# One layer of four recurrent mixers and one layer of three attentions: the gate's gelu moved and rewritten, and the last block of the memory's projection read in another order of rows

## The chip, the cores and the metric

The kernel runs on one core of one Trainium2 chip. The metric is the device time of one launch in microseconds (us), the median of several launches. Five engines work in parallel, each on its own queue of instructions in program order: TensorE (PE in the profile; PEld is its loading of weights), VectorE (DVE), ScalarE (ACT), GpSimd (POOL) and SyncE (SP, which here issues most of the DMA). An engine waits for another by a semaphore, and everything behind a waiting instruction in its own queue waits too.

## What is computed

256 tokens of width 2048 go through two blocks. The first block normalises x, projects it with `w_in` to the inputs of four mixers (gated DeltaNet, mLSTM, RG-LRU, RWKV-7), joins their outputs, projects with `w_out`, and adds a gated feed-forward network. The second block has three attentions (MoBA, dilated, memory) and a gated merge. The parts that the change touches are these:

```
def rglru_block(u, conv_w, conv_b, w_a, b_a, w_x, b_x, lam):
    xb, gate = jnp.split(u, 2, axis=-1)
    xb = causal_conv(xb, conv_w) + conv_b
    ...
    a = jnp.exp(log_a)
    inp = jnp.sqrt(-jnp.expm1(2.0 * log_a)) * (i * xb.astype(jnp.float32))
    _, h = lax.associative_scan(linear_scan_combine, (a, inp), axis=1)
    return h * jax.nn.gelu(gate.astype(jnp.float32))
...
    mix = jnp.concatenate([y.astype(x.dtype) for y in (y_gdn, y_mlstm, y_rglru, y_rwkv)], axis=-1)
    x = x + mix @ w_out[l]
...
        mkv = jnp.einsum('bmd,de->bme', mem_n, w_mem_kv[layer])
```

## The kernel before

Every large matrix product is a list of **blocks** of 512 (or twice 256) columns, and a block a list of **steps**, one for each 128 rows k of the weights. The products are in fp32 precision by splitting both operands into a high and a low part: in mode N (lines 653 to 655) a step is six matmuls 128x512, high by high, low by high, high by low, for two tiles of tokens. SyncE loads weights into `raw` (three units), ScalarE casts each half of a unit to `ringH` (line 1362), VectorE subtracts to get `ringL` (line 1983); the rings hold four halves of two steps each. The results in the two PSUM pairs `pp` are drained by ScalarE (line 1423 for the memory's values) or VectorE. The blocks' order is fixed: RWKV's inputs, mLSTM's, DeltaNet's, the RG-LRU's gate `r1` and its input `r0`, the memory's keys and values `kv0` to `kv3`, then the output projection `o0.3` to `o3.3`, `o0.1` and so on, whose number behind the dot is the mixer that it reads. A block can have a gate: `o0.3` may not begin before the stage `mix3` is open.

Beside the blocks run the **stages**, the small work of the mixers. Each stage is a generator that yields at points where other work may go in between. `course` puts the two together, in the same way for each engine. In the stretch of interest its line is

```
    L.weave(L.both(L.stage("gdn"), small_mixers(L), "rwkv"), 3.5)
```

so DeltaNet's stage is advanced by one piece, then `small_mixers` by one piece, and then `weave` gives TensorE as many steps of the blocks as the piece's pace says (3 to 5), which fill the time in which VectorE and ScalarE answer the small matmuls. If the next step's gate is closed, no step is given. DeltaNet's small matmuls are: the inversion of its triangular matrices in five levels, each with a first product (line 801, 16 of 64x64, drained by VectorE line 2260), then the second and third (line 801, 32 of 64x32, drained by lines 2268 and 2273); the join of halves (lines 865 and 871, drained by lines 2316 and 2321); and the two chunks of the recurrence (line 1171, drained by ScalarE 1780; 1178, drained by 2679; 1164, drained by 2668, 2672 and 2657; 1171 again), then the outputs (1189, 1190).

`small_mixers` holds in this order: the RG-LRU (`rglru`: per half of two tiles the convolution 2515, two products 1213, sigmoids 1816, tanh 1823, exp 1828, square 1831 and square root 1834 on ScalarE, 2716 to 2732 on VectorE), the load of x for the residual (`xload`), and then `mix3`: the splitting of RWKV's output (tiles 12 to 15 of `mix`) into high and low parts in `nS` (ScalarE 1842, VectorE 2739). `nS` holds the memory until `kv3` has read it, so `mix3` comes behind the whole of `kv3`, and all of its pieces at once (`L.run("mix3")`).

The gelu of the RG-LRU's gate lies inside `rglru`: a square on ScalarE (1802), two operations on GpSimd (2964, 2966), a tanh on ScalarE (1826) and two more on GpSimd (2976, 2978), all 128x1024 f32.

Of the kernel before, what the change touches and what calls it, by code (L numbers as in the profile page):

```python
# [9 lines left out]
ACT = mybir.ActivationFunctionType  # L10
# [6 lines left out]
T = 256  # L17
# [300 lines left out]
def program(nc, I, out):  # L318
    ctx = ExitStack()
    with ctx:  # L320
# [26 lines left out]
        def v3(o, a, b):  # L347
            return AR[:, o:o + a * b].rearrange("p (a b) -> p a b", a=a)
# [142 lines left out]
        def block(tag, W, nk, cols, x, mode="M", gate=None, by="A"):  # L491
            if mode == "M" and cols == 512:
                for name, c in (("." + tag, slice(0, 256)), (tag, slice(256, 512))):
                    block(name, W[:, c], nk, 256, x, mode, gate, by)
                return
            pos = 0
            B = Block(len(blocks), tag, W, nk, cols, mode, x, by)
            blocks.append(B)
            for u in range(0, nk, 2048 // cols):
                nu = min(2048 // cols, nk - u)  # L500
                units.append((W[128 * u:128 * (u + nu), :].rearrange("(k p) n -> p k n", p=128), nu, cols))
                for h in range(0, nu, 1024 // cols):
                    nh = min(1024 // cols, nu - h)
                    halves.append((len(units) - 1, h, nh, cols, h + nh >= nu))
                    for kk in range(nh):
                        k = u + h + kk
# [84 lines left out]
        def tensor(e, S, ring, lane):  # L591
# [527 lines left out]
            def gdn(L):  # L1119
# [77 lines left out]
                yield 5  # L1197

            def rglru(L):
                yield  # L1200
# [122 lines left out]
            def attB(L):  # L1323
# [11 lines left out]
                "norm": norm, "gates": gates, "scan": scan, "fold": fold, "lambda": lam, "stat2": stat2, "mem": mem, "rwkv": rwkv, "mlstm": mlstm, "gdn": gdn,  # L1335
                "rglru": rglru, **{f"mix{m}": split(4) for m in range(4)}, **{f"split1.{q}": split1(q) for q in range(4)},
                **{f"split2.{q}": split2(q) for q in range(4)}, "xf": split(8), "attA": attA, "attM": attM, "attB": attB,
                **{f"ysplit.{n}": ysplit(n) for n in range(5)}, "mgsplit.0": mgsplit(0, 12), "mgsplit.1": mgsplit(12, 16)}))

        def scalar(e, S, ring, lane):  # L1340
# [388 lines left out]
            def gdn(L):  # L1729
# [63 lines left out]
                yield  # L1793

            def rglru(L):
                Lp, Ln = small[:, 40:44], small[:, 48:52]
                yield
                L.upto("r0")
                GA = v3(MU, 4, T)
                e.wait_ge(*ml_v.at("end"))  # L1800
                e.wait_ge(*pool.at("r1"))
                act(GA, mix[:, 8:12, :], ACT.Square).then_inc(*rg_a.tick("sq"))
                X, Rr, Ii, Aa, Th = (v3(RU + 1040 + 512 * k, 2, T) for k in range(5))
                for hf in range(2):
# [17 lines left out]
                    for j in range(2):  # L1822
                        t = act(Th[:, j, :], Rr[:, j, :], ACT.Tanh, scale=Lp[:, 2 * hf + j:2 * hf + j + 1])
                    if hf == 0:
                        e.wait_ge(*pool.at("gl"))
                        act(GA, GA, ACT.Tanh, scale=float(np.sqrt(2.0 / np.pi))).then_inc(*rg_a.tick("th"))
                    for j in range(2):
# [107 lines left out]
            def final(L):  # L1935
# [11 lines left out]
                "norm": norm, "scan": scan, "mem": mem, "fold": fold, "lambda": lam, "rwkv": rwkv, "mlstm": mlstm,  # L1947
                "gdn": gdn, "rglru": rglru,
                **{f"mix{m}": split("mix", nS, lambda k: mix[:, k, :], range(4 * m, 4 * m + 4), mix_ready) for m in range(4)},
# [7 lines left out]
        def vector(e, S, ring, lane):  # L1957
# [636 lines left out]
            def gdn(L):  # L2594
# [107 lines left out]
                yield  # L2702

            def rglru(L):
                e.memset(rU[:, :, 0:3], 0.0).then_inc(*rg_v.tick("pad"))
# [4 lines left out]
                for hf in range(2):  # L2710
# [18 lines left out]
                    yield  # L2729
                    e.wait_ge(*pool.at("ge"))  # L2730
                    own(rg_v)
                    tt2(mix[:, 8 + 2 * hf:10 + 2 * hf, :], GA[:, s2, :], Th, MUL).then_inc(*rg_v.tick(hf, "end"))
                    yield
# [126 lines left out]
            def attB(L):  # L2860
# [6 lines left out]
            course(lane(unit, {  # L2867
                "norm": norm, "gates": gates, "scan": scan, "mem": mem, "fold": fold, "lambda": lam, "rwkv": rwkv, "mlstm": mlstm, "gdn": gdn, "rglru": rglru,
                **{f"mix{m}": split("mix", nS, lambda k: mix[:, k, :], range(4 * m, 4 * m + 4)) for m in range(4)}, "stat1": stat1,
# [6 lines left out]
        def gpsimd(e, S, ring, lane):  # L2876
# [81 lines left out]
            def rglru(L):  # L2958
                X, Rr, Ii, Aa, Th = (v3(RU + 1040 + 512 * k, 2, T) for k in range(5))
                GA, g = v3(MU, 4, T), mix[:, 8:12, :]  # L2960
                yield
                L.upto("r0")
                e.wait_ge(*rg_a.at("sq"))
                e.tensor_scalar(GA, GA, 0.044715, 1.0, MUL, ADD).then_inc(*pool.tick())
                e.wait_ge(*pool.now())
                e.tensor_tensor(GA, GA, g, MUL).then_inc(*pool.tick("gl"))
                for hf in range(2):
                    yield
                    yield
                    e.wait_ge(*rg_v.at("cv", hf, 1))  # L2970
                    e.wait_ge(*rg_a.at(hf, "g", 1))
                    e.tensor_tensor(Ii, Ii, X, MUL).then_inc(*pool.tick("ix", hf))
                    yield
                    if hf == 0:
                        e.wait_ge(*rg_a.at("th"))
                        e.tensor_scalar(GA, GA, 0.5, 0.5, MUL, ADD).then_inc(*pool.tick())
                        e.wait_ge(*pool.now())
                        e.tensor_tensor(GA, GA, g, MUL).then_inc(*pool.tick("ge"))
                    yield
                    yield  # L2980
                    yield
# [231 lines left out]
```

## Time and profile before

| | us |
|---|---|
| median of 3 runs | 2418.83 (2418.06 to 2420.80) |
| the profiled execution, whole | 2422.39 |
| its span in the profile | 2420.6 |
| TensorE busy | 2391.7 (99%) |
| VectorE busy | 1451.6 (60%) |
| ScalarE busy | 1131.5 (47%) |
| GpSimd busy | 104.1 (4%) |

The profile is one execution recorded by the hardware. "Busy" counts the time in which at least one instruction of the engine runs. A line of the timeline gives start, duration, engine, line of the kernel, operation, output and input, a count, and in brackets the idle time before it and what ended that. Lines that run back to back are merged with a count. A matmul row of count 32 at line 801 is 16 products of the program, each recorded as two passes.

### The profile page before, as it was taken

The page shows a single profiled execution, that of the slowest core. Times are in us where ns is not written, and L with a number is a line of the kernel's source. Part 1 is how long each engine was busy: PE and PEld are TensorE (multiplying, and loading weights), DVE is VectorE, ACT ScalarE, POOL GpSimd, SP SyncE. Part 2 cuts the span into 40 slices and gives each one's busy share as a digit, 9 for nine tenths or more (in the row PEclk, how much of TensorE's full clock was granted, in tenths as well). Part 3 has the DMA queues.
Part 4 walks back from the last instruction along what each step waited for, and adds up shares of the span by engine and source line. Part 5 has one row for each costly group of instructions (what it writes and reads, how often), then busy time and mean ns, then how long its engine had stood idle before and what let it go on. Part 6 is the DMA issues. An engine that isn't in the chain of part 4 may idle for free.

```text
span 2420.6 us, 32301 instructions
## 1 busy us (share of the span) xinstructions
PE 2391.7 (99%) x13432; PEld 1990.9 (82%) x13432; DVE 1451.6 (60%) x1860; ACT 1131.5 (47%) x1425; POOL 104.1 (4%) x81
## 2 busy tenths in 40 slices
PE   9999999999999999999999999999999999999998
PEld 7777888978888888888888888888888888888887
DVE  6777657678755555555555565555555655555555
ACT  6635435563554444434443464445444455444444
POOL 1000001320000000000000040000000000000000
PEclk9999999999999999999999999999999999999999
DMA  9633334645555555555555566555445544555564
GB/s 298 224 123 122 123 123 162 234 162 184 196 192 184 185 190 188 195 189 184 184 190 191 181 213 232 188 177 168 163 157 191 191 140 157 192 191 192 192 240 140
DMA packets 245329, 443.55 MB, mean 183 GB/s; under 512 B 7360, under 2 KB 72512, under 8 KB 242624
## 3 DMA queue, kind: packets, MB, share of 16 engines
q1 hardware_dynamic: 241984, 423.65, 53.2%
q0 software_dynamic: 2624, 17.30, 1.9%
q8 instruction: 107, 1.75, 0.3%
q10 hardware_dynamic: 576, 0.53, 0.1%
q14 instruction: 38, 0.31, 0.0%
HBM read 430.97 MB, written 10.49 MB: 182 GB/s over the span
## 4 chain that ended last, share of the span: by engine, by line
PE 95%; DVE 2%; ACT 1%; DMA 1%; issue 0%; SPq 0%; ACTq 0%; DVEq 0%
PE pp L653 25%; PE pp L655 24%; PE pp L654 24%; PE pp L682 8%; PE pp L683 4%; PE ps L612 2%; PE ps L1274 1%; PE ps L1288 1%; PE ps L801 1%; DVE ringL L1983 1%; DMA mem_hold<-memSt 1%; DMA raw<-in_w_in 0%; PE ps L854 0%; ACT ringH L1362 0%; PE pp L688 0%
## 5 line engine op out<-in xcount | busy, mean ns | idle before, releaser
L1983 DVE TENSOR_TENSOR ringL<-raw,ringH 128x1024 fp32r<-128x1024 f32 x779 | 963.3, 1243 | 687.8 <-ACT ringH L1362 686.3
L1362 ACT CAST ringH<-raw 128x1024 fp32r<-128x1024 f32 x779 | 814.6, 1050 | 994.9 <-PE pp L655 870.3
L653 PE MATMUL pp<-ringH,nS 128*128 128x512 f32 x1376 | 544.0, 395 | 1.1 <-DVE nS L2739 1.1
L655 PE MATMUL pp<-ringH,nS 128*128 128x512 f32 x1376 | 536.4, 390 | 0.0
L654 PE MATMUL pp<-ringL,nS 128*128 128x512 f32 x1376 | 535.9, 389 | 0.0
L682 PE MATMUL pp<-nS,ringH 128*128 128x512 f32 x992 | 367.9, 411 | 8.7 <-DVE ringL L1983 4.5
L655 PEld LDWEIGHTS pp<-ringH,nS 128*128 128x128 f32 x1376 | 258.3, 188 | 54.4
L653 PEld LDWEIGHTS pp<-ringH,nS 128*128 128x128 f32 x1376 | 258.5, 188 | 54.0 <-ACT AR L1423 1.2
L654 PEld LDWEIGHTS pp<-ringL,nS 128*128 128x128 f32 x1376 | 258.6, 188 | 51.3 <-issue 0.2
L683 PE MATMUL pp<-nS,ringL 128*128 128x256 f32 x992 | 281.4, 284 | 0.0
L653 PE MATMUL pp<-ringH,xS 128*128 128x512 f32 x704 | 277.2, 394 | 0.0
L654 PE MATMUL pp<-ringL,xS 128*128 128x512 f32 x704 | 275.2, 391 | 0.0
L655 PE MATMUL pp<-ringH,xS 128*128 128x512 f32 x704 | 274.8, 390 | 0.0
L682 PEld LDWEIGHTS pp<-nS,ringH 128*128 128x128 f32 x992 | 189.9, 191 | 58.9 <-DVE ringL L1983 7.0
L683 PEld LDWEIGHTS pp<-nS,ringL 128*128 128x128 f32 x992 | 190.8, 192 | 0.3 <-issue 0.2
L655 PEld LDWEIGHTS pp<-ringH,xS 128*128 128x128 f32 x704 | 132.1, 188 | 30.3
L653 PEld LDWEIGHTS pp<-ringH,xS 128*128 128x128 f32 x704 | 132.3, 188 | 28.3
L654 PEld LDWEIGHTS pp<-ringL,xS 128*128 128x128 f32 x704 | 132.3, 188 | 27.9
L653 PE MATMUL pp<-ringH,hS 128*128 128x512 f32 x352 | 139.9, 397 | 0.0
L654 PE MATMUL pp<-ringL,hS 128*128 128x512 f32 x352 | 138.9, 395 | 0.0
L655 PE MATMUL pp<-ringH,hS 128*128 128x512 f32 x352 | 138.9, 395 | 0.0
L2027 DVE TENSOR_TENSOR AR<-AR,pp 128x512 f32<-128x512 f32 x128 | 87.6, 687 | 37.5 <-PE pp L655 35.0
(406 smaller groups left out, 1951.5 us busy)
## 6 DMA issues: line engine op xcount, KB each, us to landing
raw<-in_w_in SPq DMA_DIRECT2D x189, 1024.0 KB, 5.1
raw<-in_ffn_w_gate SPq DMA_DIRECT2D x44, 1024.0 KB, 5.2
raw<-in_ffn_w_up SPq DMA_DIRECT2D x44, 1024.0 KB, 5.1
raw<-in_ffn_w_down SPq DMA_DIRECT2D x44, 1024.0 KB, 5.1
raw<-in_w_out SPq DMA_DIRECT2D x32, 1024.0 KB, 5.1
raw<-in_w_mem_kv SPq DMA_DIRECT2D x16, 1024.0 KB, 5.3
raw<-in_w_proj_a SPq DMA_DIRECT2D x8, 1024.0 KB, 5.0
raw<-in_w_proj_m SPq DMA_DIRECT2D x8, 1024.0 KB, 5.1
```

The lines of the kernel that those rows point to most:

```text
L612: t = e.transpose(b[:, 128 * n:128 * n + 128], s, ident)
L653: mm(o, XH[:, ts(j)], WH, first, False)
L654: mm(o, XH[:, ts(j)], WL, False, False)
L655: t_of[0] = mm(o, XL[:, ts(j)], WH, False, last)
L682: mm(bk[j], WH[:, c], nS[:, k, :, :], first, False)
L683: t = mm(bk[j][:, T:2 * T], WL[:, c], XH, False, last)
L801: t = m1(o, lhs[c][:, n, :], rhs[c][:, n, :] if b is None else rhs[c][:, n, :, :], n == 0)
L1274: t = mm(b[:, ts(m - a)], qt, kt, m == a and r == 0, r == len(scores[m]) - 1)
L1288: t = mm(b[:, 0:values[m].shape[-1]], PT[:, ts(m)], values[m], m == 0, m == n - 1)
L1362: e.copy(ringH[:, h % NSPL, 0:nh * cols], raw[:, u % NRAW, h0 * cols:(h0 + nh) * cols]).then_inc(*hi.tick(h))
L1983: tt2(ringL[:, h % NSPL, o], raw[:, u % NRAW, h0 * cols:(h0 + nh) * cols], ringH[:, h % NSPL, o].bitcast(F32), SUB).then_inc(*lo.tick(h))
L2027: tt2(x, x, bk[b][:, :], ADD).then_inc(*drain_v.tick(*name))
```

## The change

It has two parts that meet in `small_mixers`.

1. The gelu becomes a stage of its own, `gelu`, ahead of `rglru`. It begins two pieces behind the end of block `r1` and is four pieces long. Its arithmetic is now square (ScalarE), one scalar_tensor_tensor (VectorE), tanh (ScalarE), one scalar_tensor_tensor (VectorE); the factor one half goes into the RG-LRU's last multiplication. GpSimd's four operations are gone.
2. Block `kv3` reads its rows from 12 on (12 to 15, then 0 to 11), so that the tiles 12 to 15 of `nS` are free early. `mix3` may begin when 11 steps of `kv3` are left, and is now walked piece by piece (`yield from`) instead of at once.

```diff
 def small_mixers(L):
+    while not L.done("r1") and "gdn" not in L.open:
+        yield
+    yield
+    yield
+    yield from L.stage("gelu")
     while not L.done("r0") and "gdn" not in L.open:
         yield
     yield
     yield
     yield from L.stage("rglru")
     yield from L.stage("xload")
+    while L.i <= L.ends["kv3"] - 11 and "gdn" not in L.open:
+        yield
+    L.upto("kv3", -11)
+    yield from L.stage("mix3")
     while not L.done("kv3") and "gdn" not in L.open:
         yield
     L.upto("kv3")
-    L.run("mix3")
-    yield
...
-            pos = 0
+            pos, first_k = 0, 12 if tag == "kv3" else 0
...
+                k0 = (u + first_k) % nk
+                units.append((W[128 * k0:128 * (k0 + nu), :].rearrange("(k p) n -> p k n", p=128), nu, cols))
...
             def mix_ready(k):
+                e.wait_ge(*use.at(half_end["kv3"] - (7 if k >= 12 else 1)))
...
+            def gelu(L):
+                GA, g = v3(MU, 4, T), mix[:, 8:12, :]
+                yield
+                e.wait_ge(*rg_a.at("sq"))
+                stt(out=GA, in0=GA, scalar=1.0 / 0.044715, in1=g, op0=ADD, op1=MUL).then_inc(*rg_v.tick("gl"))
+                yield
+                yield
+                e.wait_ge(*rg_a.at("th"))
+                stt(out=GA, in0=GA, scalar=1.0, in1=g, op0=ADD, op1=MUL).then_inc(*rg_v.tick("ge"))
+                yield
```

What this does to the order is not in the diff. Lines of the changed kernel are shifted: 653 to 655 are 661 to 663, 801 is 809, 865 and 871 are 873 and 879, 1171, 1178 and 1164 are 1179, 1186 and 1172, 1213 is 1226.

TensorE, behind the last step of `kv3`. Before, from the join on (most rows of the blocks, which repeat, are cut):

```order
L865 MATMUL ps<-AR 64x64 x8
L653 MATMUL pp<-ringH,nS 128x512
L654 MATMUL pp<-ringL,nS 128x512
L655 MATMUL pp<-ringH,nS 128x512
...
L871 MATMUL ps<-AR 64x64 x8
...
L1171 MATMUL ps<-AR 128x128 x4
```

TensorE in the changed kernel (the first row is the last matmul of `kv3`, the last row the first of `o0.3`):

```order
L663 MATMUL pp<-ringH,nS 128x512
L809 MATMUL ps<-AR 64x64 x16
L809 MATMUL ps<-AR 64x32 x32
L873 MATMUL ps<-AR 64x64 x8
L879 MATMUL ps<-AR 64x64 x8
L1179 MATMUL ps<-AR 128x128 x4
L1186 MATMUL ps<-AR 128x128 x4
L1172 MATMUL ps<-AR 128x128 x4
L1179 MATMUL ps<-AR 128x128 x4
L661 MATMUL pp<-ringH,nS 128x512
```

Eight groups of DeltaNet's small products now follow each other with no step of a block between them; the 138 matmuls of `o0.3` and the blocks behind it that stood there, in seven portions of 12 to 30, now come later.

VectorE, last two levels of the inversion. Before:

```order
L2268 TENSOR_TENSOR AR<-AR,ps 64x8x4x8 x2
L2273 TENSOR_TENSOR AR<-AR,ps 64x8x4x8 x2
L1983 TENSOR_TENSOR ringL<-raw,ringH 128x1024 x2
L2732 TENSOR_TENSOR AR<-AR 128x512
L2260 TENSOR_TENSOR AR<-ps,cm 64x8x64 x2
L1983 TENSOR_TENSOR ringL<-raw,ringH 128x1024
L2268 TENSOR_TENSOR AR<-AR,ps 64x8x2x16 x2
L2273 TENSOR_TENSOR AR<-AR,ps 64x8x2x16 x2
L1983 TENSOR_TENSOR ringL<-raw,ringH 128x1024
L2739 TENSOR_TENSOR nS<-AR,nS 128x256 x4
L2260 TENSOR_TENSOR AR<-ps,cm 64x8x64 x2
```

VectorE in the changed kernel (2286 and 2291 are 2268 and 2273; 2278 is 2260; 2745 to 2760 are the RG-LRU's 2716 to 2732):

```order
L2745 SCALAR_TENSOR_TENSOR AR<-AR 128x512
L2747 TENSOR_SCALAR AR<-AR 128x512
L2286 TENSOR_TENSOR AR<-AR,ps 64x8x2x16 x2
L2291 TENSOR_TENSOR AR<-AR,ps 64x8x2x16 x2
L2001 TENSOR_TENSOR ringL<-raw,ringH 128x1024
L2750 SCALAR_TENSOR_TENSOR AR<-AR 128x512
L2753 TENSOR_TENSOR AR<-AR 128x512
L2756 SCALAR_TENSOR_TENSOR AR<-AR 128x256 x2
L2278 TENSOR_TENSOR AR<-ps,cm 64x8x64 x2
L2760 SCALAR_TENSOR_TENSOR AR<-AR 128x512
L2286 TENSOR_TENSOR AR<-AR,ps 64x8x32 x2
```

The RG-LRU's second half moved two levels back: its first two operations now stand ahead of the update 2286 of the fourth level, and its next four ahead of the drain 2278 of the fifth.

ScalarE, around the drain of `kv3` (1423 before, 1436 after). Before:

```order
L1831 ACTIVATE AR<-AR 128x512
L1362 CAST ringH<-raw 128x1024 x2
L1834 ACT_TABLE_LOAD
L1834 ACTIVATE AR<-AR 128x512
L1362 CAST ringH<-raw 128x1024 x3
L1423 ACTIVATE AR<-pp,small 128x512 x2
L1842 CAST nS<-AR 128x256 x4
```

ScalarE in the changed kernel (1848 and 1851 are the square 1831 and the square root 1834; 1793 is 1780; 1859 is 1842):

```order
L1848 ACTIVATE AR<-AR 128x512
L1436 ACTIVATE AR<-pp,small 128x512 x2
L1851 ACT_TABLE_LOAD
L1851 ACTIVATE AR<-AR 128x512
L1859 CAST nS<-AR 128x256 x2
L1793 COPY AR<-ps 128x512
L1859 CAST nS<-AR 128x256 x4
```

The square root of the RG-LRU's second half now stands behind the drain of `kv3`; that of the first half stands in the same way behind the drain of `kv2`.

## Rows read from the trace of the kernel before

**Rows 1.** Page: span, busy us of the engines, one group (busy, mean ns).

```profile
span 2420.6 us, 32301 instructions
PE 2391.7 (99%) x13432; PEld 1990.9 (82%) x13432; DVE 1451.6 (60%) x1860; ACT 1131.5 (47%) x1425; POOL 104.1 (4%) x81
...
L1983 DVE TENSOR_TENSOR ringL<-raw,ringH 128x1024 fp32r<-128x1024 f32 x779 | 963.3, 1243 | 687.8 <-ACT ringH L1362 686.3
```

**Rows 2.** Timeline, TensorE's stops between 460 and 640 us, and VectorE ahead of the last.

```profile
487.87 0.50 PE L682 MATMUL pp<-nS,ringH 128*128 128x512 f32 x1 [0.45 <-DVE ringL L1983]
...
491.60 1.97 PE L1213 MATMUL ps<-AR,w2s 128*128 128x256 f32 x8 [1.34 <-issue]
...
558.82 1.43 DVE L2739 TENSOR_TENSOR nS<-AR,nS 128x256 fp32r<-128x256 f32 x4 [1.07 <-ACT nS L1842]
...
559.38 0.47 PE L653 MATMUL pp<-ringH,nS 128*128 128x512 f32 x1 [1.12 <-DVE nS L2739]
```

**Rows 3.** Timeline, VectorE: two casts while GpSimd runs the gelu.

```profile
475.81 4.63 DVE L1983 TENSOR_TENSOR ringL<-raw,ringH 128x1024 fp32r<-128x1024 f32 x2 [0.70 <-ACT ringH L1362]
```

**Rows 4.** Timeline, TensorE: small products of DeltaNet, 548 to 581 us.

```profile
548.15 1.15 PE L801 MATMUL ps<-AR 64*64 64x64 f32 x32
...
553.54 2.06 PE L801 MATMUL ps<-AR 64*64 64x32 f32 x64
...
569.97 1.14 PE L865 MATMUL ps<-AR 64*64 64x64 f32 x16
...
579.28 1.05 PE L1171 MATMUL ps<-AR 128*128 128x128 f32 x8
```

**Rows 5.** Timeline, VectorE and ScalarE: what drains the small products, 560 to 598 us.

```profile
560.28 1.41 DVE L2260 TENSOR_TENSOR AR<-ps,cm 64x512 f32<-64x512 f32 x2
...
571.24 0.69 DVE L2316 COPY AR<-ps 64x512 f32<-64x512 f32 x1
...
580.37 0.59 ACT L1780 COPY AR<-ps 128x512 f32<-128x512 f32 x1 [0.54 <-PE ps L1171]
...
586.74 0.69 DVE L2679 COPY AR<-ps 128x512 f32<-128x512 f32 x1 [2.43 <-PE ps L1178]
...
594.91 1.12 DVE L2668 TENSOR_SCALAR AR<-ps,small 128x128 f32<-128x128 f32 x4
596.06 0.69 DVE L2672 TENSOR_TENSOR AR<-AR 128x512 f32<-128x512 f32 x1
596.79 0.87 DVE L2657 TENSOR_SCALAR AR<-AR,gcol 128x128 f32<-128x128 f32 x4
```

**Rows 6.** Timeline: products, square, root and drain around the RG-LRU's second half.

```profile
528.15 1.89 PE L1213 MATMUL ps<-AR,w2s 128*128 128x256 f32 x8
...
538.01 0.63 ACT L1831 ACTIVATE AR<-AR 128x512 f32<-128x512 f32 x1
...
542.01 1.28 ACT L1834 ACT_TABLE_LOAD   x1
543.30 0.63 ACT L1834 ACTIVATE AR<-AR 128x512 f32<-128x512 f32 x1
...
557.22 1.27 ACT L1423 ACTIVATE AR<-pp,small 128x512 f32<-128x512 f32 x2 [3.83 <-PE pp L655]
```

**Rows 7.** Timeline, VectorE: the RG-LRU's second half, 538 to 548 us.

```profile
539.40 0.43 DVE L2718 TENSOR_SCALAR AR<-AR 128x512 f32<-128x512 f32 x1
...
543.97 0.70 DVE L2721 SCALAR_TENSOR_TENSOR AR<-AR 128x512 f32<-128x512 f32 x1 [1.44 <-ACT AR L1834]
...
545.50 1.27 DVE L2727 TENSOR_TENSOR_SCAN AR<-AR 128x256 f32<-128x256 f32 x2
546.80 0.87 DVE L2268 TENSOR_TENSOR AR<-AR,ps 64x256 f32<-64x256 f32 x2
```

**Rows 8.** Timeline, then a window: TensorE's stop before 78.07 us; third figure from the end: granted clock.

```profile
78.07 0.50 PE L682 MATMUL pp<-nS,ringH 128*128 128x512 f32 x1 [2.66 <-DVE ringL L1983]
...
78.00:82.00 4.00, 3.93 (x13) 3.42 (x14) 3.93 (x9) 1.60 (x3) 0.00 (x0) 0.57 0.79 244
```

More of the change, by code:

```diff
@@ L505, in block @@
                     for kk in range(nh):
-                        k = u + h + kk
+                        k = k0 + h + kk
                         pos += 1
@@ L1197, in gdn @@
                 yield 5
+            def gelu(L):
+                L.upto("r1")
+                for _ in range(4):
+                    yield
             def rglru(L):
@@ L1335, in tensor @@
                 "norm": norm, "gates": gates, "scan": scan, "fold": fold, "lambda": lam, "stat2": stat2, "mem": mem, "rwkv": rwkv, "mlstm": mlstm, "gdn": gdn,
-                "rglru": rglru, **{f"mix{m}": split(4) for m in range(4)}, **{f"split1.{q}": split1(q) for q in range(4)},
+                "gelu": gelu, "rglru": rglru, **{f"mix{m}": split(4) for m in range(4)}, **{f"split1.{q}": split1(q) for q in range(4)},
                 **{f"split2.{q}": split2(q) for q in range(4)}, "xf": split(8), "attA": attA, "attM": attM, "attB": attB,
@@ L1793, in gdn, with gelu @@
                 yield
+            def gelu(L):
+                GA = v3(MU, 4, T)
+                e.wait_ge(*ml_v.at("end"))
+                e.wait_ge(*pool.at("r1"))
+                act(GA, mix[:, 8:12, :], ACT.Square).then_inc(*rg_a.tick("sq"))
+                yield
+                yield
+                e.wait_ge(*rg_v.at("gl"))
+                act(GA, GA, ACT.Tanh, scale=0.044715 * float(np.sqrt(2.0 / np.pi))).then_inc(*rg_a.tick("th"))
+                yield
             def rglru(L):
@@ L1798, in rglru @@
                 L.upto("r0")
[L1799 to L1802, printed above, removed]
                 X, Rr, Ii, Aa, Th = (v3(RU + 1040 + 512 * k, 2, T) for k in range(5))
@@ L1823, in rglru @@
                         t = act(Th[:, j, :], Rr[:, j, :], ACT.Tanh, scale=Lp[:, 2 * hf + j:2 * hf + j + 1])
-                    if hf == 0:
-                        e.wait_ge(*pool.at("gl"))
-                        act(GA, GA, ACT.Tanh, scale=float(np.sqrt(2.0 / np.pi))).then_inc(*rg_a.tick("th"))
                     for j in range(2):
@@ L1947, in scalar @@
                 "norm": norm, "scan": scan, "mem": mem, "fold": fold, "lambda": lam, "rwkv": rwkv, "mlstm": mlstm,
-                "gdn": gdn, "rglru": rglru,
+                "gdn": gdn, "gelu": gelu, "rglru": rglru,
                 **{f"mix{m}": split("mix", nS, lambda k: mix[:, k, :], range(4 * m, 4 * m + 4), mix_ready) for m in range(4)},
@@ L2702, in gdn, with gelu @@
                 yield
+            def gelu(L):
+                GA, g = v3(MU, 4, T), mix[:, 8:12, :]
+                yield
+                e.wait_ge(*rg_a.at("sq"))
+                stt(out=GA, in0=GA, scalar=1.0 / 0.044715, in1=g, op0=ADD, op1=MUL).then_inc(*rg_v.tick("gl"))
+                yield
+                yield
+                e.wait_ge(*rg_a.at("th"))
+                stt(out=GA, in0=GA, scalar=1.0, in1=g, op0=ADD, op1=MUL).then_inc(*rg_v.tick("ge"))
+                yield
             def rglru(L):
@@ L2729, in rglru @@
                     yield
-                    e.wait_ge(*pool.at("ge"))
                     own(rg_v)
-                    tt2(mix[:, 8 + 2 * hf:10 + 2 * hf, :], GA[:, s2, :], Th, MUL).then_inc(*rg_v.tick(hf, "end"))
+                    stt(out=mix[:, 8 + 2 * hf:10 + 2 * hf, :], in0=GA[:, s2, :], scalar=0.5, in1=Th, op0=MUL, op1=MUL).then_inc(
+                        *rg_v.tick(hf, "end"))
                     yield
@@ L2867, in vector @@
             course(lane(unit, {
-                "norm": norm, "gates": gates, "scan": scan, "mem": mem, "fold": fold, "lambda": lam, "rwkv": rwkv, "mlstm": mlstm, "gdn": gdn, "rglru": rglru,
+                "norm": norm, "gates": gates, "scan": scan, "mem": mem, "fold": fold, "lambda": lam, "rwkv": rwkv, "mlstm": mlstm, "gdn": gdn, "gelu": gelu, "rglru": rglru,
                 **{f"mix{m}": split("mix", nS, lambda k: mix[:, k, :], range(4 * m, 4 * m + 4)) for m in range(4)}, "stat1": stat1,
@@ L2959, in rglru @@
                 X, Rr, Ii, Aa, Th = (v3(RU + 1040 + 512 * k, 2, T) for k in range(5))
-                GA, g = v3(MU, 4, T), mix[:, 8:12, :]
                 yield
                 L.upto("r0")
[L2963 to L2966, printed above, removed]
                 for hf in range(2):
@@ L2973, in rglru @@
                     yield
[L2974 to L2978, printed above, removed]
                     yield
```

1 line of the change is left out of this document (removed).

## The prediction

> **What bounds the kernel now.** I read the page's first part, then TensorE's own stops in the timeline, then the granted clock. TensorE is busy 2391.7 of 2420.6 us [rows 1], so it sets the end, and a change is worth only what it adds to or takes from TensorE's stops. VectorE (1451.6 us), ScalarE and GpSimd have slack on the whole and matter only where TensorE waits for them. In the stretch that the change touches, 460 to 640 us, TensorE stops three times [rows 2]: 0.45 us for a cast of VectorE, 1.34 us ahead of the RG-LRU's first products (line 1213), 1.12 us for the first split tile of RWKV's output. That is 2.9 us, 0.12% of the time, and it is all that the change can win there. Everywhere else in the stretch the small products of DeltaNet leave no stop, since steps of the blocks stand between them: from the first product of a level at 548.15 to the next small product at 553.54 there are 5.4 us, of which the product itself takes 1.1 and 18 matmuls of a block 4.3 [rows 4], while VectorE's drain takes 1.41 [rows 5].
>
> **What the change removes.** The RG-LRU's first products are asked for two levels later, when their convolution is long done, so the 1.34 us go. GpSimd's four operations on 128x1024 go. While they run, VectorE is slow: two casts take 4.63 us [rows 3] where one takes 1.24 on the mean [rows 1]. So the 0.45 us, whose cast stands behind that, go too. The two new VectorE operations on 128x1024 are each about 1.24 us by the cast of the same size, 2.5 us together in a stretch where VectorE has gaps; the tanh on ScalarE is followed by DeltaNet's exponential, for which no other table is loaded in between in the new order, so its load of 1.28 is not one more. I cost the gelu at nothing: TensorE has two steps and more of cast weights ahead of it there. If that cover failed, it would cost at most those 2.5 us. `mix3` is split before `o0.3` is asked for, so the 1.12 us go as well. Sum of this part: -2.9 us.
>
> **What it adds: the order without filling.** The gelu's four pieces come before the RG-LRU, which therefore ends later; the walk of `mix3` piece by piece takes four more pieces of DeltaNet. By the order of the instructions, the steps of `kv3` are used up before that, and `o0.3` may not begin until `mix3` is open. So `weave` has nothing to give, and eight groups of small products stand in a row, from the last level's first product to the recurrence's second chunk. Each now has to wait for its drain in full. I take 0.1 us for one hand-over between engines, an estimate: VectorE's first of four pieces that begin at 558.82 (1.43 in all, so 0.36 each) ends at 559.18 and TensorE starts at 559.38, and within other pairs it is less [rows 2].
>
> Term D, the tail. The join's first product is drained in 0.69, the second by an operation of the same size, again 0.69; the recurrence's first product by ScalarE in 0.59, the state by VectorE in 0.69, and the fourth product by 1.12, 0.69 and 0.87 in a row [rows 5]. That is 5.3 us, with two hand-overs at each of the five places 6.3 us of stops. Between the last level's second products and the join there is none: the join waits only for the first half of them.
>
> Term C, the last level. Its first product (1.1 us) must be drained by 2260, but in VectorE's order four operations of the RG-LRU stand ahead of that, the first of which needs the square root, and ScalarE's order puts this root behind the drain of `kv3`. I set the clock at the end of the RG-LRU's second products. Before, these ended at 528.15+1.89=530.04 and the square (1831) at 538.64 [rows 6], 8.6 us later; the same operations stand between them now, with one cast more, which falls into a wait. Then ScalarE: drain 1.27, table load 1.28, root 0.63 [rows 6], done at 11.8. VectorE: 0.70 and 0.43, the update 0.87 (done at 10.7), its twin 0.87, a cast 1.24, so 12.8, then 0.70, 0.69 (the size of 2316), the scans 1.27 and the drain 1.41 [rows 1, 5, 7]: 16.9. TensorE can begin the first product at 10.8 and ends it at 11.9. Stop: 5.0 us.
>
> Term B, the level before. The update 2268, on which the last level's first product waits, stands behind the RG-LRU's operations that need the square: 8.6+0.70+0.43+0.87+0.15=10.8. TensorE's own work from the same point is a product with 18 matmuls (5.4), the second products 2.06, and the last six matmuls of `kv3` 1.4, together 8.9 [rows 4]. Stop: 1.9 us.
>
> Term A, the RG-LRU's first half, two levels in. Here the root stands behind the drain of `kv2`: 1.27+1.28+0.63 on ScalarE, 0.70+0.69+1.27+1.41 on VectorE [rows 5 to 7], with hand-overs 7.4 us, against 5.4 us of product and filling. Stop: 2.0 us.
>
> A bound for A and B from below is nothing, if the casts between let ScalarE through earlier; for C it is the drain alone, 1.41+0.2=1.6; for D the operations without hand-overs, 5.3. From above, double hand-overs add 1 us to D and little to the others.
>
> Term E, the clock. After a stop of 2.66 us the granted clock was 0.57 on the mean of the next four us [rows 8]: up to 0.43x4=1.7 us lost, between the levels of 2.4 and 1.2 GHz. The new stops of 5.0 and of 2.9 us (the last in D) are longer. Two falls at 1.4 us, somewhat under the bound because small products do not all hang on the array: 2.8 us. The bound below is 0.
>
> Sum: -2.9+2.0+1.9+5.0+6.3+2.8=+15.1 us. The matmuls that moved behind DeltaNet cost nothing there; TensorE does them in any case, and it has no stop there now that they could fill. Against the profiled execution (span 2420.6, 2422.39 in all, 3.6 above the median) this is a span of 2435.7; against the median of the three runs, 2418.83, it gives **2434 us**.
>
> One rule is weighed against this. In the trace the operation behind a table load begins at once: load at 542.01 for 1.28, root at 543.30 [rows 6]. The Trainium skill, page "ScalarE: Activation LUTs", section "What ACT_TABLE_LOAD costs", counts a drain of about 1380 ns on top of the load for every switch. A and C have one load each on their path; by the page the sum would be 2.8 us more. The row shows no such gap, so I stay with the row.
>
> **Rivals.**
>
> 1. *Only the tail counts* (about 2424). ScalarE and VectorE run the RG-LRU early enough that A and B vanish and C is its drain alone. Then -2.9+1.6+6.3=+5.0, 2423.8. For it: in the kernel before the same work never stopped TensorE. Against it: the new order puts the root behind the drain of a block that ends just then, which a row can't outrun.
>
> 2. *The clock stays low through the whole tail* (2441). TensorE's work between the stops is 2.06+2x1.14+4x1.05=8.5 us [rows 4]; at half the clock it could take twice that. Then the sum is 12.3 (without E) + 8.5 + 1.4 for the steps behind it = +22.2, 2441. For it: in the tail TensorE works about half of the time. Against it: the small products are short and not all bound by the array. The Trainium skill, page "TensorE: Matmul & The Clock Gate", section "Part 1: The HAM clock gate", says that the throttled state is the default and activity releases it; that would give this rival its time. The trace agrees in one place, the stop before 78.07 us, but there TensorE had dense work behind it.
>
> 3. *Faster* (2416). The one mechanism: VectorE, freed of GpSimd's contention in this stretch (4.63 us for two casts that take 2.5), and the three stops removed, 2.9 us, against a row of small products whose stops are hidden. It decides at 2.9 us: if the seven hand-overs cost less than 0.4 us each, the kernel is not slower. That would need products that don't wait for the drains of 0.59 to 2.7 us that they read, so I see it only if TensorE's steps are not where the order puts them, that is, if the change doesn't do what its order says.
>
> **How the numbers follow.** Forecast 0.72, rival 1 0.10, rival 2 0.14, rival 3 0.04. The time is the forecast's, 2434. Its own lower bound is without A, B, E and the hand-overs, +7.4, 2426; upwards rival 2 with double hand-overs, 2443. From 2426 to 2443 leaves out rivals 1 and 3 and a few hundredths of the ends. A measurement of this kernel can tell about 0.2% (4.8 us) from no change; rival 1 lies at that border and is shared between same and slower. So faster 0.03, same 0.06, slower 0.91.
>
> **What the profile after would show.** TensorE's three stops of 0.45, 1.34 and 1.12 us gone; five new stops of 0.8 to 2.9 us at the join and the recurrence, all within 15 us, ended by VectorE (one by ScalarE); one of about 5 us ahead of the last level's second products and one of 2 us ahead of its first, with the RG-LRU's scans and the drain of `kv3` in the chain; one of 2 us at the second level; a granted clock near one half in windows behind the long ones; TensorE's busy time nearly unchanged, 2389 to 2400. GpSimd's busy time down by about 8 us. The forecast is wrong if steps of a block stand between the small products of the tail, or if the stops there sum to less than 5 us.

## The result: 21.9 us slower

| | us |
|---|---|
| before, median | 2418.89 |
| changed kernel, median of 4 runs | 2440.76 (2439.25 to 2442.25) |
| ratio | 1.0089, 95% interval 1.0077 to 1.0101 |
| profiled execution of the changed kernel, whole | 2439.25 |
| its span | 2437.5 |

The forecast was 2434 us, with a range from 2426 to 2443. The page of the changed kernel, as in [rows 1]:

```profile
span 2437.5 us, 32314 instructions
PE 2394.5 (98%) x13432; PEld 1994.6 (82%) x13432; DVE 1451.3 (60%) x1862; ACT 1131.9 (46%) x1425; POOL 94.2 (4%) x77
```

TensorE has the same 13432 matmul records and is busy 2.8 us longer; its idle time, the span less the busy time, grew from 28.9 to 43.0 us. GpSimd lost 9.9 us, VectorE is unchanged. The waits of TensorE between 480 and 600 us say where the idle time is (columns: who waited for what, total, times, longest). Of the three stops of [rows 2] none is left:

```profile
PE ps L809 <- DVE AR L2278: 7.3, 2, 5.1
PE ps L1179 <- DVE AR L2675: 2.9, 1, 2.9
PE ps L809 <- DVE AR L2286: 2.1, 1, 2.1
PE ps L879 <- DVE AR L2334: 0.9, 1, 0.9
PE ps L1172 <- DVE AR L2697: 0.9, 1, 0.9
PE ps L1179 <- DVE AR L2339: 0.9, 1, 0.9
PE ps L1186 <- ACT AR L1793: 0.8, 1, 0.8
```

The timeline of TensorE puts them in order, and shows a second thing. The same products that took 2.06, 1.14 and 1.05 us before [rows 4] take 3.30, 1.94 and 2.04 to 2.05 from 562 us on:

```profile
523.58 2.50 PE L809 MATMUL ps<-AR 64*64 64x32 f32 x64 [2.23 <-DVE AR L2278]
...
556.02 1.15 PE L809 MATMUL ps<-AR 64*64 64x64 f32 x32 [2.12 <-DVE AR L2286]
562.28 3.30 PE L809 MATMUL ps<-AR 64*64 64x32 f32 x58 [5.11 <-DVE AR L2278]
...
568.14 1.94 PE L879 MATMUL ps<-AR 64*64 64x64 f32 x16 [0.88 <-DVE AR L2334]
570.94 2.04 PE L1179 MATMUL ps<-AR 128*128 128x128 f32 x8 [0.87 <-DVE AR L2339]
573.75 2.05 PE L1186 MATMUL ps<-AR 128*128 128x128 f32 x8 [0.77 <-ACT AR L1793]
...
581.62 2.05 PE L1179 MATMUL ps<-AR 128*128 128x128 f32 x8 [2.90 <-DVE AR L2675]
```

The table by stretches of the changed kernel explains that. Its columns are the stretch and its length, the busy us of PE, PEld, DVE, ACT and POOL with the number of instructions, the granted clock, the DMA share and GB/s. To compare: behind the stop at 78 us the mean was 0.57 over four us [rows 8].

```profile
525.00:527.00 2.00, 2.00 (x24) 1.78 (x21) 1.87 (x5) 0.00 (x0) 0.00 (x0) 0.50 0.55 101
527.00:529.00 2.00, 2.00 (x7) 1.58 (x6) 1.36 (x2) 0.16 (x1) 0.00 (x0) 0.65 1.04 397
...
558.00:560.00 2.00, 0.00 (x0) 0.00 (x0) 1.86 (x4) 0.00 (x0) 0.00 (x0) 0.78 0.05 18
560.00:580.00 20.00, 13.05 (x120) 11.94 (x120) 10.05 (x25) 1.80 (x5) 0.00 (x0) 0.50 0.27 106
...
582.00:586.00 4.00, 4.00 (x14) 3.44 (x14) 0.92 (x2) 1.53 (x2) 0.00 (x0) 0.50 0.00 0
586.00:588.00 2.00, 2.00 (x9) 1.62 (x8) 0.49 (x1) 0.15 (x1) 0.00 (x0) 0.90 0.14 18
```

Between 531 and 558 us the clock is full. It is at its lower level, 1.2 GHz, from 559 us to 586, through the whole tail and the first three us of `o0.3`, which begins at 583.3.

The chain behind the 5.11 us stop, in VectorE's timeline: the RG-LRU's operations stand ahead of the drain 2278, and VectorE works without a gap from the square on.

```profile
553.82 0.69 DVE L2745 SCALAR_TENSOR_TENSOR AR<-AR 128x512 f32<-128x512 f32 x1 [5.03 <-ACT AR L1848]
...
557.95 0.68 DVE L2750 SCALAR_TENSOR_TENSOR AR<-AR 128x512 f32<-128x512 f32 x1
...
560.77 1.41 DVE L2278 TENSOR_TENSOR AR<-ps,cm 64x512 f32<-64x512 f32 x2
```

The two spans differ by only 16.9 us, since the profiled execution of the kernel before lay 3.5 us above its median and that of the changed kernel 1.5 below. The traces show where most of this comes from. Ahead of the stretch that the change touches, the granted clock fell five times in the kernel before (at 78, 283, 297, 304 and 427 us) and twice in the changed one (at 78 and 211), and each fall costs about 1.7 us. So the stretch is better measured by itself, between two groups of small products that stand in both kernels at the same place of TensorE's order. Before, then in the changed kernel:

```profile
452.05 1.47 PE L612 MATMUL ps<-cm,AR 128*128 128x128 f32 x12
...
658.18 0.60 PE L612 MATMUL ps<-cm,AR 128*128 128x128 f32 x4
```

```profile
447.58 1.47 PE L620 MATMUL ps<-cm,AR 128*128 128x128 f32 x12
...
675.03 0.60 PE L620 MATMUL ps<-cm,AR 128*128 128x128 f32 x4
```

That is 206.13 us before and 227.45 after, 21.3 us more, close to the 21.9 between the medians. From the second of these groups to TensorE's last matmul both take the same 1754.7 us. The whole loss lies in the stretch.

Two executions, one of e4 (3970.6 us) and one of e7 (2970.5 us), ran at a mean clock of 0.56 and 0.75 throughout, and the medians and ratios below leave them out.

### The profile page after: what moved, and what is told of

Its sections match the earlier page's. It is cut to its first block, busy times and chain, and to the rows that moved or that the text cites. A ratio compares the mean times of both kernels' runs of the same rounds, so it can differ in the third digit from the quotient of the medians.

```text
span 2437.5 us, 32314 instructions
## 1 busy us (share of the span) xinstructions
PE 2394.5 (98%) x13432; PEld 1994.6 (82%) x13432; DVE 1451.3 (60%) x1862; ACT 1131.9 (46%) x1425; POOL 94.2 (4%) x77
## 4 chain that ended last, share of the span: by engine, by line
PE 94%; DVE 3%; ACT 1%; DMA 1%; issue 0%; SPq 0%; ACTq 0%; DVEq 0%
PE pp L661 24%; PE pp L663 24%; PE pp L662 24%; PE pp L690 8%; PE pp L691 4%; PE ps L620 2%; PE ps L1287 1%; PE ps L1301 1%; PE ps L809 1%; DVE ringL L2001 1%; DMA mem_hold<-memSt 1%; DMA raw<-in_w_in 0%; ACT ringH L1375 0%; PE ps L862 0%; PE pp L696 0%
## 5 line engine op out<-in xcount | busy, mean ns | idle before, releaser
L690 PE MATMUL pp<-nS,ringH 128*128 128x512 f32 x992 | 362.3, 406 | 9.3 <-DVE ringL L2001 4.1
```

Of the source, the lines that this page charges most:

```text
L690: mm(bk[j], WH[:, c], nS[:, k, :, :], first, False)
```

## The experiments

**The theory**: the stops, by the order of the instructions, cost about 13 us; they make the clock fall, and that costs the rest, 9 to 10. Rivals: the new arithmetic or `kv3`'s order of rows costs by itself; the clock is low for another reason than the stops; the small products are bound by their drains, so that their length doesn't matter.

All runs in one table. Differences are between medians of the same set of runs. The last column is the stretch between the two groups of small products named above, in the one profiled execution of each run, against the 206.1 us of the kernel before; falls of the clock elsewhere don't enter it.

| | us | before | difference | ratio, 95% interval | stretch |
|---|---|---|---|---|---|
| changed kernel | 2440.76 | 2418.89 | +21.9 | 1.0089 (1.0077 to 1.0101) | +21.3 |
| e1 gelu's part alone | 2433.28 | 2419.42 | +13.9 | 1.0053 (1.0041 to 1.0066) | +12.6 |
| e2 rows' part alone | 2427.54 | 2419.42 | +8.1 | 1.0031 (1.0019 to 1.0042) | +8.1 |
| e3 `mix3` at once | 2430.29 | 2419.42 | +10.9 | 1.0049 (1.0035 to 1.0062) | +12.0 |
| e4 gelu beside, `mix3` early | 2416.89 | 2419.42 | -2.5 | 0.9988 (0.9979 to 0.9997) | -2.5 |
| e5 the last six stops filled | 2433.12 | 2419.92 | +13.2 | 1.0054 (1.0040 to 1.0067) | +14.3 |
| e6 only the long one filled | 2440.74 | 2419.92 | +20.8 | 1.0083 (1.0069 to 1.0096) | +18.6 |
| e7 only the tail's filled | 2438.98 | 2419.92 | +19.1 | 1.0075 (1.0061 to 1.0089) | +18.9 |
| e8 new gelu beside, alone | 2417.37 | 2420.45 | -3.1 | 0.9992 (0.9983 to 1.0001) | -2.1 |
| e9 `mix3` early, old gelu | 2419.74 | 2420.45 | -0.7 | 0.9996 (0.9987 to 1.0005) | -0.4 |

### Each part alone, and the walk by pieces (e1, e2, e3)

e1 is the changed kernel with the old handling of `kv3` and `mix3`:

```diff
-            pos, first_k = 0, 12 if tag == "kv3" else 0
+            pos, first_k = 0, 0
...
-    while L.i <= L.ends["kv3"] - 11 and "gdn" not in L.open:
-        yield
-    L.upto("kv3", -11)
-    yield from L.stage("mix3")
     while not L.done("kv3") and "gdn" not in L.open:
         yield
     L.upto("kv3")
+    L.run("mix3")
+    yield
...
-                e.wait_ge(*use.at(half_end["kv3"] - (7 if k >= 12 else 1)))
+                e.wait_ge(*use.at(half_end["kv3"] - 1))
```

> The gelu's part of the change alone: the stage gelu with its two VectorE and two ScalarE operations; kv3 keeps its rows from 0 on and mix3 is run at once behind kv3, as before. TensorE's order: the RG-LRU's products stand where they stand in the changed kernel, the last level's second products and the join's second product have no step of a block ahead of them, but the recurrence has steps (12, 30, 24, 24 matmuls) again. Theory (filling decides): the stops of 2.2, 2.1 and 5.1 us stay, one of 0.9 at the join, the recurrence has none, the one for mix3's first tile (1.1) is there; the granted clock falls behind the 5.1 us stop but is full again a few us later. 2418.9 - 1.8 + 10.3 + 4 to 5 for the clock = about 2432. Rival 1 (the rows' part and the walk by pieces cost the time, the gelu nothing): 2417 to 2420. Rival 2 (once fallen, the clock stays at half to 587 us whatever TensorE does): 2437 or more.

e2 is the kernel before with the opposite edit, the old gelu and the new `kv3` and `mix3`.

> The rows' part alone, on the kernel before: kv3 from row 12 on, mix3 may begin 11 steps before its end and is walked piece by piece; the gelu is the old one with GpSimd. TensorE's order: RG-LRU's products as in the kernel before; last level's second products, the join's and the recurrence's first product bare, then 24, 30 and 18 matmuls of the blocks ahead of the next ones. Theory: the stop for mix3 (1.12) is gone; the last level's drain alone is waited for (1.6), two stops of 0.9 in the tail; no stop over 2 us, so at most one short fall of the clock: 2418.9 - 1.1 + 3.4 + 0 to 3 = 2421 to 2424. Rival (most of the 22 us come from this part, since it takes mix3's filling away): 2430 or more.

e3 is the changed kernel with one line changed:

```diff
-    yield from L.stage("mix3")
+    L.run("mix3")
+    yield
```

> The changed kernel with one edit: mix3 run at once instead of piece by piece. TensorE's order is then that of the run with the gelu's part alone; only kv3's rows and the moment from which mix3 may begin differ. Theory: the recurrence's four stops (0.87, 0.77, 0.88, 2.90) and the half clock behind 575 us go, the stops of 2.2, 2.1, 5.1 and 0.9 stay: about 2431, some 10 us under the changed kernel and within 1.5 of the run with the gelu's part alone. Rival (clock once fallen stays low; stops in the recurrence were covered by it): 2437.

**Measured.** +13.9, +8.1 and +10.9 us. The two parts together give 22.0, the changed kernel 21.9, but that they add up so well is chance: both runs have a stop at the last level and one at the join, and neither has the three stops of 0.77, 0.88 and 2.90 us in the recurrence. TensorE's waits from 480 to 600 us in e1, then in e2:

```profile
PE ps L807 <- DVE AR L2276: 7.0, 2, 4.8
PE ps L807 <- DVE AR L2284: 2.1, 1, 2.1
PE ps L877 <- DVE AR L2332: 0.9, 1, 0.9
```

```profile
PE ps L804 <- DVE AR L2264: 2.5, 1, 2.5
PE ps L1216 <- issue: 1.3, 1, 1.3
PE ps L874 <- DVE AR L2320: 0.9, 1, 0.9
PE ps L1174 <- DVE AR L2325: 0.9, 1, 0.9
PE pp L685 <- DVE ringL L1987: 0.5, 1, 0.5
```

e1 is 1.3 us above its expectation. The stops are those that were named, without the one for `mix3`. What the expectation had wrong is the clock, which was to be full again a few us behind the long stop: it is at 0.61 from 560 to 562 us, at 0.50 up to 576 and at 0.63 from 576 to 578. The gelu's part brings the stops of 2.2, 2.1 and about 5 us, by its place and not by its arithmetic (e8, below). It lets the RG-LRU end two levels later. Both rivals of e1's expectation (2417 to 2420, 2437 or more) are out.

e2 was expected at 2421 to 2424 and missed that by 3.5. Its longest stop is 2.5 us instead of 1.6: VectorE's first split of `mix3` now stands ahead of the drain 2264 and waits for ScalarE, which had the drain of `kv3` until 554.4 and its cast behind that:

```profile
554.77 0.42 DVE L2743 TENSOR_TENSOR nS<-AR,nS 128x256 fp32r<-128x256 f32 x1 [1.06 <-ACT nS L1845]
```

And its clock, table by stretches:

```profile
559.00:569.00 10.00, 8.25 (x66) 7.55 (x64) 4.95 (x14) 1.53 (x2) 0.00 (x0) 0.50 0.25 97
```

The clock is at the lower level for some 14 us (557 to 571), from just behind the stop of 2.5 us on, with the two of 0.9 within. With a stop of 0.46 at 603 us, outside the list above, TensorE's stops come to 6.5 us. That accounts for 6.5-2.9=3.6 us of the 8.1; the other 4.5 are left for the clock.

e3 came out as expected (2431, measured 2430.3). With steps of the blocks back in the recurrence, four of the five stops of the tail are gone, and the clock rises at 573 us instead of 587:

```profile
560.00:572.00 12.00, 8.62 (x100) 8.09 (x101) 9.12 (x20) 0.14 (x1) 0.00 (x0) 0.50 0.47 176
572.00:574.00 2.00, 2.00 (x8) 1.53 (x8) 0.98 (x3) 0.00 (x0) 0.00 (x0) 0.76 0.24 23
```

The four stops sum to 5.4 us (0.87, 0.77, 0.88, 2.90), and one of 0.46 at 610 us is new; e3 lies 10.5 us under the changed kernel by the medians and 9.3 in the stretch. About half is the clock's. That the clock once fallen stays low to 587 us whatever TensorE does, e3's rival, is out.

### Stops or clock (e5, e6, e7)

These three put matmuls without a use into the stops, so that only TensorE's idle time changes and the order and the drains don't.

```diff
+            def fill(place):
+                i = ends["kv3"] + 1
+                B, h = steps[i].block, steps[i].half
...
+                for _ in range(FILL[place]):
+                    m1(PS[2 * (B.n % 2)][:, :], ringH[:, h % NSPL, 0:128], ringH[:, h % NSPL, 0:512], True)
...
+                    if lv == 4 and mp is gd_p:
+                        fill("C")
                     for c in range(2):
                         e.wait_ge(*mv.at(*key, "t1", lv, c))
...
```

The same call stands ahead of five more waits, one in the join and four in the recurrence. The matmuls run on weights that are there, and the first matmul of `o0.3` resets the bank that they write.

> The changed kernel with matmuls that compute nothing needed (128x512, weights of o0.3's first half by themselves, into the PSUM bank that o0.3's first matmul resets) put ahead of six waits: 20 ahead of the last level's second products (the 5.1 us stop), 3 each ahead of the join's second product, the recurrence's first, second and third, 11 ahead of its fourth (the 2.9 us stop). At full clock they take 0.21 us each and fit into the stops (4.3, 0.6, 0.6, 0.6, 0.6, 2.4 us). Theory A (the stops make the clock fall, and the small products then take twice as long): the clock stays full from 559 to 588 us, the small products take 1.05 us instead of 2.04, and the time is some 8 us under the changed kernel: about 2433. Theory B (the fall has another cause than idle time): the 43 matmuls run at half clock, 18.5 us in stops of 10.7: about 2449. Theory C (the time of the tail is the drains' alone): 2440 to 2441.

> As the run before, but only the 20 matmuls ahead of the last level's second products. Theory A1 (the one stop of 5.1 us makes the fall; the tail's short stops do nothing by themselves): the clock stays full to the end of the tail, about 2434, as with all filled. Theory A2 (the tail's sparse products are enough): the clock is full to about 570 us and falls within the tail; most of the loss is there again, 2437 to 2440.

> As the first of these three, but only the 23 matmuls in the join and the recurrence; the 5.1 us stop is left bare. The clock falls there as in the changed kernel. Theory A: with TensorE at work without a gap from 562 us on, the clock comes back within the tail, after some of the matmuls have run at half of it; 2436 to 2440. If it stays at half to 587 us all the same: 23 x 0.43 = 9.9 us in 6.3 us of stops, so 2444.

**Measured**, e5: 2433.1, as theory A said, 7.6 us under the changed kernel (8.7 by the differences to the kernel before, 7.0 in the stretch) although TensorE has 43 matmuls more to do. Its table by stretches, and its small products:

```profile
558.00:560.00 2.00, 2.00 (x12) 1.59 (x10) 1.90 (x3) 0.67 (x3) 0.00 (x0) 0.50 0.52 199
560.00:562.00 2.00, 2.00 (x8) 1.57 (x8) 1.94 (x4) 0.00 (x0) 0.00 (x0) 0.75 0.00 0
562.00:580.00 18.00, 17.58 (x168) 13.99 (x167) 11.08 (x29) 2.85 (x7) 0.00 (x0) 1.00 0.31 118
```

```profile
564.33 1.93 PE L822 MATMUL ps<-AR 64*64 64x32 f32 x59
...
570.00 1.13 PE L1198 MATMUL ps<-AR 128*128 128x128 f32 x8
571.80 1.16 PE L1206 MATMUL ps<-AR 128*128 128x128 f32 x8
...
577.76 1.16 PE L1198 MATMUL ps<-AR 128*128 128x128 f32 x8 [0.34 <-DVE AR L2695]
```

From the last level's second products to the end of the recurrence's fourth it is 564.33 to 578.92, 14.6 us; in the changed kernel it is 562.28 to 583.67, 21.4. The 6.8 us between them are the length of the same products at the lower clock: the time from the end of a product to the start of the next hardly differs, 0.67 us from 571.13 to 571.80 where the changed kernel waits 0.77. Theories B and C are out. In detail one thing differs from the expectation: the first third of the 20 matmuls ran at half clock, since the clock had already fallen behind the stop of 2.12 us ahead of them. So the second products begin 7.4 us behind the start of the first (556.94 to 564.33), and 6.3 in the changed kernel; e5 pays 1.1 us for that.

e6: 2440.7, no gain by the median (+20.8 where the changed kernel has +21.9). But in the stretch it is 2.7 us shorter than the changed kernel; its profiled execution (2439.9 us) had four falls of the clock ahead of the stretch where the changed kernel's (2439.3) had two, and these hide the gain there. Whether they do in its other executions isn't shown. Behind the stop of 2.12 us the clock was low to 563 us. From 564 to 572 us it is full, and then it falls within the tail, where no stop had been over 0.9 us:

```profile
572.00:574.00 2.00, 1.50 (x8) 1.24 (x8) 0.64 (x2) 0.01 (x1) 0.00 (x0) 0.76 0.49 201
574.00:586.00 12.00, 7.50 (x28) 6.71 (x29) 4.81 (x14) 3.12 (x7) 0.00 (x0) 0.50 0.00 1
```

That is theory A2. In this trace no long stop was needed ahead of the second fall; a row of short ones between small products was enough. e7: 2439.0, and 2.4 us shorter than the changed kernel in the stretch. TensorE works almost without a gap from 564.6 us on, and the clock comes back between 578 and 579:

```profile
563.00:577.00 14.00, 12.38 (x112) 10.96 (x113) 6.74 (x16) 0.59 (x2) 0.00 (x0) 0.50 0.40 152
577.00:579.00 2.00, 2.00 (x11) 1.86 (x10) 0.43 (x1) 1.21 (x4) 0.00 (x0) 0.63 0.00 0
```

That is theory A, inside its range of 2436 to 2440: counted from the start of the last level's second products, the clock is full some 10 us earlier than in the changed kernel, but by then the first 9 extra matmuls had been paid at half of it. In the stretch each of the two partial fillings gains about 2.5 us and the whole one 7.0, more than the two together.

### The same work in another place (e4, e8, e9)

e4 keeps the new arithmetic and `kv3`'s new order, and gives the gelu's pieces together with the RG-LRU's; `mix3` comes as soon as it may:

```diff
-    while not L.done("r1") and "gdn" not in L.open:
-        yield
-    yield
-    yield
-    yield from L.stage("gelu")
...
-    yield from L.stage("rglru")
+    gelu = L.stage("gelu")
+    for _ in L.stage("rglru"):
+        next(gelu, None)
+        yield
+        if "mix3" not in L.open and L.i > L.ends["kv3"] - 11:
+            L.run("mix3")
...
```

> The changed kernel with the gelu's pieces given together with the RG-LRU's instead of ahead of them, and mix3 run at once as soon as 11 steps of kv3 are left, inside the RG-LRU's stage if it comes to that. The new gelu arithmetic and kv3's order of rows are kept. TensorE's order: RG-LRU's products where they are in the kernel before, and 12 to 30 matmuls of the blocks ahead of every small product of the tail. Theory: all seven new stops go, the clock stays full from 500 to 590 us, GpSimd's contention and the stop for mix3 are gone: 2416 to 2419, level with the kernel before or just under. Rival (the new arithmetic on VectorE costs by itself): 2422 or more.

e8 has the first of these two edits on e1, so its matmuls stand in the order of the kernel before; e9 has the second on e2.

> The new gelu arithmetic alone (two VectorE and two ScalarE operations, none on GpSimd), its pieces given together with the RG-LRU's, kv3 and mix3 as in the kernel before. TensorE's order is then that of the kernel before, matmul by matmul. Theory (the arithmetic costs nothing; GpSimd's contention goes): the stop of 0.45 us goes, that of 1.34 shrinks to about 0.2 as in the run with both (e4), that of 1.12 for mix3 stays; a stop of 0.7 us like that run's may come at the third level: 2418.0 to 2419.5, no difference from before that can be measured. Rival (most of e4's gain over before is the arithmetic): 2417. Rival (the arithmetic on VectorE costs by itself): 2422 or more.

> kv3's rows from 12 on, and mix3 run at once as soon as 11 steps of kv3 are left, inside the RG-LRU's stage if it comes to that; the gelu is the old one with GpSimd. TensorE's order is that of e4, with 12 to 30 matmuls ahead of every small product of the tail. Theory: the stop of 1.12 us goes and nothing takes its place; the other two stay; the clock stays full: 2418.3, and 9 us less than the run with the rows' part as the change makes it (2427.5), since only the walk by pieces and mix3's late place are gone. Rival (reading kv3 from row 12 on costs by itself, for instance in its weights' order of loads): 2422 or more.

**Measured.** e4 is 2.5 us faster than the kernel before, 0.12% by the ratio, the interval just clear of one, and 2.5 us shorter in the stretch. e8 is 3.1 us faster by the medians (1.9 by the ratio, 2.1 in the stretch), e9 0.7, and both intervals hold one. TensorE's waits, e4, then e8, then e9:

```profile
PE ps L810 <- DVE AR L2279: 0.7, 1, 0.7
PE ps L1227 <- issue: 0.2, 1, 0.2
```

```profile
PE pp L657 <- DVE nS L2764: 1.1, 1, 1.1
PE ps L1222 <- issue: 0.2, 1, 0.2
```

```profile
PE ps L1220 <- issue: 1.3, 1, 1.3
PE ps L808 <- DVE AR L2268: 0.7, 1, 0.7
PE pp L689 <- DVE ringL L1991: 0.5, 1, 0.5
```

The stops are 0.9, 1.3 and 2.5 us where the kernel before has 2.9, and the clock is 1.00 in each from 500 to 600 us. The new arithmetic is what takes away the stops of 0.45 and most of 1.34; the early `mix3` takes away the 1.12 and brings a 0.7. Neither costs anything by itself: the rivals that said so (2422 or more) are out. e9 against e2, both with the old gelu: 8.8 us (from +8.1 to -0.7) for the place of `mix3` alone, given at once and early instead of by pieces and late. e4 has the same operations as the changed kernel, and from +21.9 to -2.5 they are 24.4 us apart.

## Why the prediction was right, and where it was not

The sign held, and so did the mechanism of the stops; the mechanism of the clock in the tail did not, and the value was 6.8 us too low. That 2440.8 lies inside the range is owed to its upper end, which was rival 2's.

- **What goes, -2.9.** Right: the three stops of [rows 2] are gone. For the 1.34 us the reason given, that the RG-LRU's products come two levels later, isn't needed: in e8 they stand where they stood, and 0.19 us are left. The casts of [rows 3] also ran beside an operation of GpSimd that isn't the gelu's (474.10 to 477.37). The gelu's two VectorE operations took 1.22 and 2.31 us instead of 1.24 each, the second begun while an operation of GpSimd ran (464.12 to 466.33), and TensorE didn't wait for either.
- **Term D, 6.3.** Measured 0.88+0.87+0.77+0.88+2.90=6.3. The drains of [rows 5] and 0.1 us for a hand-over were enough (the 0.2 that [rows 2] shows for one would have been too much), and the stops are the same at full clock in e6 (0.89 and 0.87).
- **Term C, 5.0.** Measured 5.11. The chain is the one in the text; VectorE's own work from the square on (553.82 to 562.18) sets it, and the root was done (557.15) before VectorE came to need it (557.95).
- **Term B, 1.9, and term A, 2.0.** Measured 2.12 and 2.23. Together the stops come to 15.8 us, forecast 15.2. e8 and e4 show their cause: with the RG-LRU two levels earlier none of them is there, except 0.7 us.
- **Term E, 2.8: the term that was mis-sized.** Its step "two falls at 1.4 us", from the 0.57 over four us of [rows 8], holds for A alone: 0.50 and 0.65 in two stretches of 2 us, so 1.0+0.7=1.7 us. Behind the stop at 78 us and behind A, TensorE had dense work, and the clock was back within four us. In the tail it hadn't. There the clock cost 6.8 us in the products (e5) and 1.4 in the first 24 matmuls of `o0.3`, which took 7.0 us from 583.32 and take 5.6 in e5. That is 1.7+6.8+1.4=9.9 us in all. The step that failed is the second of the two falls: 1.4 us were put down for it, 8.2 were measured.
- **Rival 2** was the mechanism that came about, the lower clock through the whole tail. Its 8.5 us for the products was somewhat high (6.8: a part of them was short also at half clock, 3.30 for 2.06, 1.94 for 1.14), and its 1.4 for the steps behind is what was measured. Its 2441 is the measured time. It had 0.14; the argument against it, that small products are not all bound by the array, was the wrong one: they took 1.6 to 1.95 times as long. The rule weighed beside it, the Trainium skill, page "TensorE: Matmul & The Clock Gate", section "Part 1: The HAM clock gate", that the throttled state is the default and activity releases it, agrees with e5 to e7: the clock rose only where TensorE's gaps were closed.
- **The table load.** ScalarE at term A: drain 516.00, load 517.29 for 1.28, root 518.58. The operation behind a load again begins at once; the 1380 ns more per switch that the Trainium skill gives (page "ScalarE: Activation LUTs", section "What ACT_TABLE_LOAD costs") are not there in this kernel either.
- **Rivals 1 and 3** are out by A, B and C, and by the stops of the tail, eight new ones in all.

The sum with the measured terms is 15.8-2.9+9.9=22.8 us; the medians differ by 21.9 and the stretch by 21.3. A part of the 1 to 1.5 us between them may be that eight groups in a row break into the large matmuls in seven places less. In the changed kernel the small group behind the matmul at 509.28 starts 0.32 us after it, where a large one starts 0.23 after another, and the first large one behind the group holds the next up by 0.34 instead of 0.23. That is 0.2 us a group, 1.4 for seven, an estimate that no run tests. The rest of the scatter is the clock elsewhere, about 1.7 us for each fall, which differs from one execution to the next.

Left open: e4's gain over the kernel before is settled only as far as its interval and one trace go, and whether e8 or e4 is the better isn't.

## What to carry to other kernels

Small dependent matmuls cost little as long as steps of a big product stand between them. A piece of side work that is moved ahead of them, or a gate that closes a few steps too early, takes this filling away: look in the order of the instructions for places where two small products follow each other, and price each with the whole drain between them. Then price their own length at half the clock too, and that of the steps right behind them, since a row of stops of 0.9 us each was enough to bring the clock down, and filling a part of the stops gained about 2.5 us where filling them all gained 7.0. To see differences of this size, compare the stretch between two rows that both traces have, beside the medians.

## What the chip showed that was not expected

- Between small products with stops of 0.77 to 0.89 us the granted clock fell from 1.00 to 0.50 (e6, between 572 and 574 us). In the changed kernel it was low for 27 us, and rose between 586 and 588; the last stop ended at 581.6.
- Behind a stop of 2.12 us the clock fell even with TensorE's work closed up right behind it (e5: 0.50 at 558 to 560, 1.00 from 562 on); after a stop of 0.68 us in dense work (e4) there was none. But the length of one stop doesn't settle it. A stop of 2.15 us at 210 us, untouched by the change, stands in every trace; behind it the clock fell in the changed kernel (0.74 from 210 to 212 us), e3, e6 and e9, and stayed at 1.00 in the kernel before, e1, e2, e4, e5, e7 and e8.
- VectorE is slow beside other operations of GpSimd than the gelu's too. In the changed kernel, without the gelu's four, two casts still took 3.77 us where two alone take 2.36 (516.16), beside another operation of GpSimd (128x1024, 3.38 us from 470.85). Not every pair is slow: the drain 2278, which reads PSUM, kept its 1.41 us at 546.12 beside an operation of GpSimd from 545.97.

```profile
472.68 3.77 DVE L2001 TENSOR_TENSOR ringL<-raw,ringH 128x1024 fp32r<-128x1024 f32 x2 [0.69 <-ACT ringH L1375]
```
